# Embedding LayerNorm in one VectorE pass per token tile, and a sum of squares in two accumulating parts

## The reference

```
h = layernorm(x, emb_ln_g, emb_ln_b)                # the embedding LayerNorm
for l in range(2):                                  # hybrid layers
    proj = h @ w_in[l]                              # latents, gates, pool and conv inputs
    ... mix = [attention, pool, conv] * silu(gates)
    h = layernorm(DEEPNORM_ALPHA * h + mix @ w_out[l] + b_out[l], ln_g[l], ln_b[l])
x = h
x = x + 0.5 * swiglu(rms_norm(x, ffn1_norm), gate, up, down)
x = x + mixed_attentions(rms_norm(x, mix_norm), mem) @ w_out
x = x + 0.5 * swiglu(rms_norm(x, ffn2_norm), gate, up, down)

def layernorm(x, g, b):
    mu = mean(x); var = mean((x - mu) ** 2)
    return (x - mu) * rsqrt(var + 1e-5) * g + b
def rms_norm(x, g):
    return x * rsqrt(mean(x * x) + 1e-6) * g
```

## Time and profile before

| | us |
|---|---|
| median of three executions | 2580.84 |
| lowest and highest | 2580.39, 2581.54 |
| the profiled execution | 2581.86 |
| its span | 2580.1 |
| TensorE busy | 2560.2 |
| VectorE busy | 1780.8 |
| ScalarE busy | 1360.2 |
| GpSimd busy | 17.0 |

### The profile page before, as it was taken

The page is one execution under the profiler, slowest core; times in us unless marked ns, Lnnn a source line. Parts: engine busy times, 40 slices in busy tenths (PEclk is TensorE's granted clock), DMA queues, the critical chain, the costliest instruction groups (busy, mean ns, idle before and its releaser), DMA issues.

```text
span 2580.1 us, 39872 instructions
## 1 busy us (share of the span) xinstructions
PE 2560.2 (99%) x14224; PEld 2218.3 (86%) x14224; DVE 1780.8 (69%) x2712; ACT 1360.2 (53%) x2111; POOL 17.0 (1%) x20
## 2 busy tenths in 40 slices
PE   7999999999999999999999999999999999999999
PEld 6888888888888888888888887888888888888888
DVE  8787658777658766556666765678766665666755
ACT  6665565565566444444444555775544444444443
POOL 2000000000000000000000000000000000000000
PEclk9999999999999999999999999999999999999999
DMA  7554555454554554555554564444455555555454
GB/s 296 187 188 176 184 208 228 151 190 178 181 210 164 195 194 174 184 200 194 194 185 169 191 210 159 147 151 172 179 191 188 195 169 187 211 185 194 173 182 166
DMA packets 75435, 482.41 MB, mean 187 GB/s; under 512 B 8384, under 2 KB 10816, under 8 KB 30784
## 3 DMA queue, kind: packets, MB, share of 16 engines
q1 hardware_dynamic: 75328, 481.00, 52.1%
HBM read 477.82 MB, written 2.10 MB: 186 GB/s over the span
## 4 chain that ended last, share of the span: by engine, by line
PE 83%; DVE 1%; ACT 1%; issue 0%; ACTq 0%; DVEq 0%
PE acc L809 45%; PE acc L810 23%; PE acc L815 3%; PE acc L817 3%; PE acc L816 3%; PE score L809 1%; PE score L1077 1%; PE score L810 1%; PE head_ps L1100 0%; PE turn_ps L1086 0%; PE head_ps L1101 0%; DVE low L1527 0%; PE sums L1020 0%; ACT high L1156 0%; ACT L1438 0%
## 5 line engine op out<-in xcount | busy, mean ns | idle before, releaser
L809 PE MATMUL acc<-xs,high 128*128 128x512 f32 x4000 | 1401.2, 395 | 2.5 <-DVE xs L2019 2.2
L1527 DVE TENSOR_TENSOR low<-raw,high 128x1024 fp32r<-128x1024 f32 (+2 forms) x976 | 1079.9, 1124 | 453.6 <-ACT high L1156 429.5
L1156 ACT ACTIVATE high<-raw 128x1024 fp32r<-128x1024 f32 (+2 forms) x976 | 945.3, 976 | 506.6 <-PE acc L810 376.2
L810 PE MATMUL acc<-xs,low 128*128 128x256 f32 x4000 | 1115.2, 279 | 0.0
L809 PEld LDWEIGHTS acc<-xs,high 128*128 128x128 f32 x4000 | 749.8, 187 | 175.1 <-DVE xs L2019 3.1
L810 PEld LDWEIGHTS acc<-xs,low 128*128 128x128 f32 x4000 | 753.8, 188 | 0.6
L809 PE MATMUL acc<-hidden,high 128*128 128x512 f32 x1408 | 488.3, 392 | 0.0
L1197 ACT ACTIVATE lowsum<-acc 128x256 f32<-128x256 f32 x347 | 133.2, 384 | 515.1 <-PE acc L810 514.8
L810 PE MATMUL acc<-hidden,low 128*128 128x256 f32 x1408 | 392.1, 279 | 0.0
L809 PEld LDWEIGHTS acc<-hidden,high 128*128 128x128 f32 x1408 | 263.6, 187 | 59.5
L810 PEld LDWEIGHTS acc<-hidden,low 128*128 128x128 f32 x1408 | 265.2, 188 | 0.0
(11 more groups left out here) (378 smaller groups left out, 2018.9 us busy)
## 6 DMA issues: line engine op xcount, KB each, us to landing
raw<-w_up_dram SPq DMA_DIRECT2D x176, 1024.0 KB, 4.8
raw<-w_down_dram SPq DMA_DIRECT2D x128, 704.0 KB, 4.0
raw<-w_in_dram SPq DMA_DIRECT2D x78, 1024.0 KB, 4.8
raw<-w_out_dram SPq DMA_DIRECT2D x32, 1024.0 KB, 4.8
raw<-w_heads_dram SPq DMA_DIRECT2D x24, 1024.0 KB, 4.8
raw<-w_mixout_dram SPq DMA_DIRECT2D x16, 1024.0 KB, 4.8
raw<-w_mem_dram SPq DMA_DIRECT2D x8, 1024.0 KB, 4.8
raw<-w_nat_dram SPq DMA_DIRECT2D x8, 1024.0 KB, 4.8
```

Of the source, the lines that this page charges most:

```text
L809: eng.matmul(bank_, hi, moving, start=start, stop=False)
L810: return eng.matmul(bank_[:, S:2 * S], lo, moving[:, 0:S], start=False, stop=stop)
L1156: eng.activation(high[:, s % SPLIT, to:to + n * P], raw[:, s % RAW, at_:at_ + n * P], ACT.Copy).then_inc((highs_a, highs_b)[piece], 1)
L1527: eng.tensor_tensor(low[:, s % SPLIT, w], raw[:, s % RAW, at_:at_ + n * P], high[:, s % SPLIT, w].bitcast(F32), ALU.subtract).then_inc((lo ...
```

## The change

Statistics of the embedding: for each token tile VectorE runs `bn_stats` on four chunks of 512 columns and one `bn_aggr` over their results, which give mean and variance; then it takes variance plus epsilon, ScalarE the root, VectorE the reciprocal and the bias, tile by tile, with semaphores of their own for tile 0. ScalarE's squares go. All four chunks of tile 0's `z` are written by ScalarE as soon as tile 0 is known; of tile 1, chunks 0 and 1 are VectorE's and chunks 2 and 3 ScalarE's. TensorE transposes tile 0 and tile 1 of a chunk apart.

First splits: `low` of slab 1's first half is written by GpSimd, at the head of its program, and counted in `emb_low`, for which TensorE waits before the first product with slab 1. `lows_a` isn't raised for slab 1; slab 2's first half raises it by two. The second halves of slabs 0 and 1 are split at j = 4 and j = 6, on both engines.

Second LayerNorm: VectorE stops at two folded tiles. TensorE multiplies both by the ones and accumulates: the first at the start of the fourth slab of `up10`, the second (`factor_rest`) in its middle. `ACC_AT` counts the accumulations anew, since the embedding has none.

```diff
-ACC_AT = {"emb": 0, "memory": 4, "ln0": 12, "ln1": 30, "memory_heads": 48}
+ACC_AT = {"memory": 0, "ln0": 8, "ln1": 26, "memory_heads": 44}
+FIRST_ON_DVE = 2
+    steps[("up10", LATE - 1)].append(("factor_rest",))
 # TensorE
-                            if b % 8 == 0:
+                            if b % 8 == 0 and (r.name, b) == ("in_a0", 0):
+                                eng.wait_ge(lows_a, 1)
+                            elif b % 8 == 0:
                                 eng.wait_ge((lows_a, lows_b)[b // 8], s + 2)
+                        elif (r.name, b) == ("in_a0", 0):
+                            eng.wait_ge(emb_low, 1)
+                elif kind == "factor_rest":
+                    eng.matmul(sums[:, S:2 * S], ones, square[:, 1, :], start=False, stop=True).then_inc(sumsq, 1)
+                if name == "ffn1":
+                    eng.matmul(sums[:, S:2 * S], ones, square[:, 0, :], start=True, stop=False)
+                    return
+            def turn_tile(c, b):
+                for j in (2 * c, 2 * c + 1):
+                    for m in range(2):
+                        kt = 2 * j + m
+                        last = eng.transpose(turn_banks[j % 4][:, m * S + b * P:m * S + (b + 1) * P],
+                                             z[:, b, kt * P:(kt + 1) * P], ident)
+                    if b:
+                        last.then_inc(turned_x, 1)
+            def turn_first(c):
+                if c >= 2:
+                    eng.wait_ge(split_l, split_count("emb", 4 * (c - 2) + 3))
+                    eng.wait_ge(emb_first, c + 1)
+                    turn_tile(c, 0)
+                if c < FIRST_ON_DVE:
+                    eng.wait_ge(z_done, c + 1)
+                else:
+                    eng.wait_ge(z_second, c + 1 - FIRST_ON_DVE)
+                turn_tile(c, 1)
             def between(name):
                 if name == "in_a0":
+                    eng.wait_ge(par_in, 16)
+                    for c in range(2):
+                        eng.wait_ge(emb_first, c + 1)
+                        turn_tile(c, 0)
                     turn_chunk("emb", 0)
                     turn_chunk("emb", 1)
 # ScalarE
-                    whole_squares()
+                    eng.wait_ge(emb_var, 1)
+                    eng.activation(ln_root[:, 0:1], ln_var[:, 0:1], ACT.Sqrt).then_inc(emb_root, 1)
+                    eng.wait_ge(emb_scaled, 1)
+                    for c in range(4):
+                        scaled(0, name, c).then_inc(emb_first, 1)
+                    eng.wait_ge(variance, N_OF[name] + 1)
+                    eng.activation(ln_root[:, 1:2], ln_var[:, 1:2], ACT.Sqrt).then_inc(root, 1)
+                    split_high(0, r, 0, None)
+                    split_high(0, r, 1, None)
...
                         if j in (2, 4):
                             second_scaled(name, j // 2 + 1)
-                            split_high(1, r, j // 2 - 1, None)
+                        if j in (4, 6):
+                            split_high(1, r, j // 2 - 2, None)
 # GpSimd
+            eng.wait_ge(highs_a, 2)
+            eng.tensor_tensor(low[:, 1, 0:8 * P], raw[:, 1, 0:8 * P], high[:, 1, 0:8 * P].bitcast(F32),
+                              ALU.subtract).then_inc(emb_low, 1)
 # VectorE
+                both = (s, piece) == (2, 0)
+                if both:
+                    eng.wait_ge(emb_low, 1)
                 eng.tensor_tensor(low[:, s % SPLIT, w], raw[:, s % RAW, at_:at_ + n * P], high[:, s % SPLIT, w].bitcast(F32),
-                                  ALU.subtract).then_inc((lows_a, lows_b)[piece], 1)
+                                  ALU.subtract).then_inc((lows_a, lows_b)[piece], 2 if both else 1)
-                    whole_sums()
...
+                    for b in range(TB):
+                        row_moments(b)
+                        one = slice(b, b + 1)
+                        eng.tensor_scalar(ln_var[:, one], emb_stat[:, b, 1:2], LN_EPS, None, ALU.add)\
+                            .then_inc((emb_var, variance)[b], 1)
+                        step_(eng.tensor_scalar(ln_offset[:, one], emb_stat[:, b, 0:1], -1.0, None, ALU.mult))
+                        eng.wait_ge((emb_root, root)[b], 1)
+                        step_(eng.reciprocal(ln_inv[:, one], ln_root[:, one]))
+                        eng.tensor_tensor(ln_bias[:, one], ln_offset[:, one], ln_inv[:, one], ALU.mult)\
+                            .then_inc((emb_scaled, ln_scaled)[b], 1)
+            def row_moments(b):
+                for c in range(4):
                     if c % 2 == 0:
+                        eng.wait_ge(x_in[2 * b + c // 2], 16)
+                    eng.bn_stats(emb_parts[:, b, c, :], x_tok[:, b, 512 * c:512 * (c + 1)]).then_inc(emb_moments, 1)
+                eng.wait_ge(emb_moments, 4 * (b + 1))
+                step_(eng.bn_aggr(emb_stat[:, b, :], emb_parts[:, b, :, :].rearrange("p c n -> p (c n)")))
                 if name == "emb":
+                    z_chunk(name, 1)
                     split_low(0, r, 0, None)
-                    z_chunk(name, 1)
-                    split_low(0, r, 1, None)
                     eng.wait_ge(par_in, 16)
...
-                        if j in (2, 4):
-                            z_chunk(name, j // 2 + 1)
-                            split_low(1, r, j // 2 - 1, None)
+                        if j in (4, 6):
+                            split_low(1, r, j // 2 - 2, None)
-                    step_(eng.tensor_tensor(fold, fold, square[:, 2:4, :], ALU.add))
-                    added("ffn1", eng.tensor_tensor(moment[:, S:2 * S], square[:, 0, :], square[:, 1, :], ALU.add), True)
+                    added("ffn1", eng.tensor_tensor(fold, fold, square[:, 2:4, :], ALU.add), True)
```

More of the change, by code:

```diff
@@ L376, in build @@
         ln_stat = at("ln_stat", [P, 19, TB], F32)
+        emb_parts = at("emb_parts", [P, TB, 4, 6], F32)
+        emb_stat = at("emb_stat", [P, TB, 2], F32)
         dummy = at("dummy", [P, 1], F32)
@@ L422, in build @@
         x_in = [sem(f"x_in{n}") for n in range(2 * TB)]
-        x_first, x_sums = sem("x_first"), sem("x_sums")
+        emb_moments, emb_var, emb_root, emb_scaled, emb_first, emb_low = (
+            sem(n) for n in ("emb_moments", "emb_var", "emb_root", "emb_scaled", "emb_first", "emb_low"))
         mem_tok_in, mem_h, mem_l, mem_var, mem_root, mem_scaled, mem_normed, mem_turned = (
@@ L1119, in turn_chunk @@
                 n = LAYER_NORMS.index(name)
-                if name == "emb" and c == 0:
-                    eng.wait_ge(par_in, 16)
-                eng.wait_ge(z_done, 5 * n + c + TB)
+                if name == "emb":
+                    return turn_first(c)
+                eng.wait_ge(z_done, FIRST_ON_DVE + 5 * (n - 1) + c + TB)
                 if c:
-                    eng.wait_ge(z_second, 3 * n + c)
+                    eng.wait_ge(z_second, 4 - FIRST_ON_DVE + 3 * (n - 1) + c)
                 for j in (2 * c, 2 * c + 1):
@@ L1269, in layer_norm @@
                     split_high(1, fill, 1, None)
-                eng.wait_ge(variance, N_OF[name] + 1)
-                eng.activation(ln_root, ln_var, ACT.Sqrt).then_inc(root, 1)
-                if name == "emb":
-                    split_high(0, r, 0, None)
-                    split_high(0, r, 1, None)
-                    second_scaled(name, 1)
-                    eng.wait_ge(par_in, 16)
-                else:
+                    eng.wait_ge(variance, N_OF[name] + 1)
+                    eng.activation(ln_root, ln_var, ACT.Sqrt).then_inc(root, 1)
+                if name != "emb":
                     split_high(0, fill, 2, None)
@@ L1331, in layer_norm, with scaled @@
                         eng.activation(square[:, 4 * q4:4 * q4 + 4, :], x[:, 4 * q4:4 * q4 + 4, :], ACT.Square).then_inc(squared, 1)
+            def scaled(b, name, c):
+                w = slice(512 * c, 512 * (c + 1))
+                return eng.activation(z[:, b, w], token_major(name)[:, b, w], ACT.Identity, bias=ln_bias[:, b:b + 1],
+                                      scale=ln_inv[:, b:b + 1])
             def second_scaled(name, c):
                 eng.wait_ge(ln_scaled, LAYER_NORMS.index(name) + 1)
[L1335 to L1345 removed]
+                scaled(1, name, c).then_inc(z_second, 1)
             def do(kind, *a):
```

40 lines of the change are left out of this document (2 added, 38 removed).

## The result

| | before | after |
|---|---|---|
| median, us | 2581.19 (6 runs) | 2596.93 (6 runs) |
| lowest and highest | 2578.58, 2582.87 | 2594.94, 2608.99 |
| profiled execution | 2581.86 | 2596.57 |
| its span | 2580.1 | 2594.7 |

The ratio is 1.0074, with its 95% interval 1.0052 to 1.0097. The forecast was 2580.4 in a range up to 2582.3. The six runs after don't lie around one value: four are between 2594.9 and 2597.3, two at 2607.6 and 2609.0.

A forecast was written before the change was run, and what follows sets the result against it. The prediction took TensorE, busy 99% of the span, as the bound, with 15.6 us of waits to win from. It summed -0.8 us in the prologue and +0.4 in the second LayerNorm to -0.4: 2580.4 us, range 2578.9 to 2582.3.

The forecast's parts named there:

- Statistics: Embedding prologue: eight `bn_stats` at 0.62 us each replace eight sums; first `z` of tile 1 at 11.4 us.
- The lock: First splits: GpSimd's 2.6 us `low` waits for VectorE until 13.6, then holds VectorE's `xs` subtraction to 16.2; first product 17.0.
- the slower rival (GpSimd first): First splits: GpSimd takes the port before VectorE's `low` of slab 0; +1.5 us in all, 2582.3; chance 0.15.
- The prediction's other figure, 2.3 to 2.4: GpSimd's 1024-column subtraction in us, estimated from the Trainium skill's 4497 ns for 2048 columns; first product then at 16.8.
- The clock: Rival: TensorE, standing from 14.0 to 17.0, starts its products at 1.2 GHz; b = 8 at 27.0, 2581.0 us; chance 0.17.
- The gain at b = 8: Prologue's end, from which TensorE never idles again: 26.4 us, held by `low`, against 27.19, a gain of 0.8.
- the 27.6: Sign of failure in the prologue: b = 8 later than 27.6 us would make the whole forecast wrong.
- `rows`: 3 MB load issued at 30.9 us, not 25.5, landing at 44.3; VectorE stands 3.5, TensorE doesn't wait.
- Second LayerNorm: Near 814 and 817 us: a second float32 product costs TensorE 0.43, one VectorE addition saves 0.05; cost 0.4 us.
- Behind b = 8 all waits are relative to TensorE as now: After the prologue: the 0.8 us gained at b = 8 carries on, with TensorE's later waits unchanged relative to it.
- the rule of the first part: Whole kernel: the change wins only from TensorE's 15.6 us of waits; instructions added to TensorE elsewhere cost their full time.
- All that was idle is 15.6 us: Bound on TensorE's idle time, 4.4 us of it the first DMA; chances 0.01 faster, 0.97 same, 0.02 slower.

The follow-up runs named there:

- after_again: The changed kernel, unaltered, run again: 12 runs, 5 at 2579.6 to 2582.5 us, 5 at 2592.6 to 2595.5, 2 at 2607.9 and 2609.5.
- after_warm: Changed kernel plus 22 identity transposes on TensorE ahead of the first product: 2 runs below 2586 us, 7 at 2591 to 2598, 3 above 2604.
- emb_only: Kernel before with the embedding part of the change alone, second LayerNorm's sum as before: median 2606.97 us, none of 6 runs below 2586.
- emb_dve: emb_only with the first `low` of slab 1 back on VectorE instead of GpSimd: median 2607.97 us, ratio 1.0071, 11 runs.
- after_nudge: Changed kernel plus one 64-column product ahead of the second FFN's sum-of-squares product: 6 runs below 2586 us, 4 at 2591 to 2598, 2 above 2604.
- after_wait: Changed kernel plus one satisfied TensorE wait ahead of the first product: 5 runs below 2586 us, 3 at 2591 to 2598, 4 above 2604.
- before_wait: Kernel before plus one satisfied TensorE wait ahead of the first product: 11 of 12 runs below 2586 us, 1 at 2591 to 2598.
- ffn1_only: Kernel before with the second LayerNorm part of the change alone, embedding as before: median 2582.30 us, ratio 1.0010, 12 runs.
- after_redraw: Changed kernel plus 59 small float32 products of 64 columns, one per turn of the FFN loops: 6 runs, 2612.2 to 2613.7 us.
- after_order: Changed kernel with products alternating 512, 256, 256, 512 columns in the looped slabs: median 2588.90 us, 12 runs between 2586.6 and 2592.0.

## Why the prediction was wrong

*Statistics: right.* Four `bn_stats` took 2.46 us, 0.615 each; the forecast was 0.62. VectorE's timeline, after:

```profile
6.88 1.29 DVE L2026 BATCH_NORM_STATS2 emb_parts<-x_tok 128x6 f32<-128x512 f32 x2 [1.20 <-DMA x_tok<-x_dram]
...
9.27 2.46 DVE L2026 BATCH_NORM_STATS2 emb_parts<-x_tok 128x6 f32<-128x512 f32 x4
...
12.84 1.00 DVE L2019 TENSOR_SCALAR z<-x_tok,ln_stat 128x512 f32<-128x512 f32 x2
```

In this execution the second piece of x was 1.20 us late, so `z` came at 12.84; in that of after_again there was no such wait and it came at 11.58 (forecast 11.4). The first product was at 17.79 here and at 16.53 there (forecast 17.0).

*The lock: right, its size by luck.* VectorE's pair waited for GpSimd's end, and GpSimd came second, so the slower rival (GpSimd first) did not happen. The record of 2.63 us beside the forecast 2.6 is luck: the forecast let the 2.6 begin where VectorE's `low` ends, and from there it was 2.21. The prediction's other figure, 2.3 to 2.4, was nearer. (Its GpSimd row of 0.73 is an addition, not a subtraction.)

*The clock: the rival's slow start happened, not for its reason.* "If they start at 1.2 GHz" came true in the changed kernel, but the clock had not risen before the standing (nor in the kernel before during its transposes, as the prediction has it: all 16 are at the slow rate, the products behind them at the fast one), and three executions without the embedding part start as slowly (after_warm, above).

*The gain at b = 8: not found.* It was forecast at 26.4, 0.8 ahead of 27.19, and came at 27.66, past the 27.6 that the prediction had named as a sign of being wrong. In the eight other executions with GpSimd's split and without the added transposes it came at 26.40 to 28.23, and in the four others without the embedding part at 26.57 to 27.46: medians of all, 26.8 and 26.9. So the first product did come earlier (16.5 to 17.1 in those eight, against 17.1 to 17.8 without the embedding part), but at b = 8 hardly anything of it was left. This is at most a microsecond.

*`rows`: right.* It was issued at 32.2 (forecast 30.9), VectorE stood 3.64 us (forecast 3.5) at 45.27 and not 41.52, and TensorE didn't wait:

```profile
45.27 2.29 DVE L1800 SCALAR_TENSOR_TENSOR rows<-rows 128x2048 f32<-128x2048 f32 x1 [3.64 <-DMA rows<-rows_dram]
```

*Second LayerNorm: right in kind and size.* The two products stand at 814.58 and 817.84. Each puts off what follows it by 0.43 us (0.22 for its first pass, 0.03 for its second, and the 512-column product behind it takes 0.42 until the next start and not 0.23), where one such product of 0.43 stood before:

```profile
814.58 0.59 PE L1127 MATMUL sums<-square,par 128*128 128x256 f32 x2
...
817.84 0.59 PE L1008 MATMUL sums<-square,par 128*128 128x256 f32 x2
```

*The step that failed* is the sentence "Behind b = 8 all waits are relative to TensorE as now", and with it the rule of the first part that the change can win only what it takes from the waits and that each added instruction "costs its full time". Both hold TensorE's pace as given wherever it doesn't wait. It isn't: two FFNs, each at 22.19 or 22.61 us a turn, are worth 14 us each, some 35 times the sum of -0.4. The range was built from the prologue's cases, so it had no term for this (its upper end was also drawn without the 0.7 us that the executions lie above their median; 2583.0 would not have held 2596.93 either). "All that was idle is 15.6 us" was no bound for the slower side, and holds for the prologue alone: TensorE idles 1.2 us more behind it, and 3.1 behind its last product. That the three runs of the kernel before lay within 1.2 us hid it: its share of slow FFNs is small (13 of 110 runs).

The forecast's own sum of -0.4 us is not contradicted, which is not much: +0.3 between the two kernels in the order without steps, where about a microsecond either way can't be told, and the lowest step of after_again at 2580.6 beside 2581.0 for the kernel before. What decides the median is the share of runs in which an FFN falls into the slow pace. With the embedding part (after, after_again, emb_only, emb_dve, after_nudge, after_wait, after_warm) 18 of 71 runs lay on the lowest step; without it and without a small product more at 1850 us (before, before_wait, ffn1_only) 117 of 134.

*What stays open.* Why this part, over by 30 us, makes the slow pace likelier at 818 us is not shown. It isn't GpSimd (emb_dve), nor the place in the program (before_wait, after_wait), nor a fixed property of the changed code (after_again), and keeping the clock up does not mend it (after_warm). That the point of the rhythm sets the pace behind a small product is shown in after_redraw. That a few nanoseconds do it at the entries of the FFNs is read from the traces afterwards, without a run of its own: where the sum's product comes behind the same point of the slow cycle (last gap 0.361), it goes on fast when it starts 353 ns behind the last 512-column product (before, before_wait, at 1850 us) and slow at 355 (after_wait, emb_only; twice in after_redraw); two points further on, fast at 366 (before, before_wait and ffn1_only at 818 us) and slow at 361 (after at 1850 us, emb_dve twice). At the point between them 351 stands on both sides, so one nanosecond of resolution is too coarse there. To arrive fast doesn't settle it: at 1850 us four of four go on fast (after_again, ffn1_only, after_nudge, after_warm), at about 815 us four turn slow (after, emb_only, after_nudge, after_warm). How the embedding part moves these points was not followed through the 800 us. Nor is shown what inside TensorE makes the cycle of three pairs.

## What to carry to other kernels

Where one engine is busy 99% of the time, look at its rate (instructions per 100 us in the windows, or the time of a loop's turn) before and after, ahead of its waits: a changed rate far from the edit says that the edit is not what you measure. Repeat the kernel unchanged, and look at the runs one by one: a median of a kernel whose runs lie on steps moves with their shares, and six runs can't price an edit of half a microsecond. To price one, take the steps away in both kernels (here by the order of the products), even at the cost of some microseconds.

## What the runs showed of the hardware

- Pairs of a 512- and a 256-column product, each with its own weights, run at 0.347 or 0.353 us, both steady over 700 us at a granted clock of 1.00. A small float32 product between them can turn one pace into the other, and which comes out went by its place in a cycle of three pairs, 59 times of 59 (after_redraw); the order 512, 256, 256, 512 has one pace (22.29 us a turn for 22.19 and 22.61), and 512, 512, 256, 256, the same cycle shifted, nearly so.
- A 64-column float32 product between such pairs costs 0.22 us (22.41 for 22.19 over 64 pairs), a 256-column one 0.43.
- A GpSimd subtraction of 128x1024 took 2.35 us alone (after_order) and 2.63 where it began during a two-input subtraction of VectorE; VectorE's pair beside it took 2.10, undisturbed 1.43, and its first half ended 0.54 to 0.55 us behind GpSimd's end in ten executions of ten.
